# A long and a short product of each weight block, side by side instead of in two runs

## What is computed

```python
def _swiglu(x, w_gate, w_up, w_down):
    g = jnp.einsum('bsd,df->bsf', x, w_gate)
    u = jnp.einsum('bsd,df->bsf', x, w_up)
    return jnp.einsum('bsf,fd->bsd', jax.nn.silu(g) * u, w_down)

def first_block(x, ...):
    for layer in range(DEPTH):                 # DEPTH = 2
        ...
        x = _layer_norm(DEEPNORM_ALPHA * x + mix, ln1_g[layer], ln1_b[layer])
        ffn = _swiglu(x, ffn_w_gate[layer], ffn_w_up[layer], ffn_w_down[layer])
        x = _layer_norm(DEEPNORM_ALPHA * x + ffn, ln2_g[layer], ln2_b[layer])
    return x

def second_block(x, mem, ...):
    h = rms_norm(x, norm_g[layer])
    (qa, ka, va, ga, ub, vb, gb, qc, gc, ma, mb, mc) = split_cols(h @ w_in[layer], IN_SPLITS)
    ...
```

## Time and profile before

| | us |
|---|---|
| median of 3 runs | 916.92 |
| lowest and highest run | 916.55, 918.35 |
| span of the profiled execution | 915.3 |

### The profile page before, as it was taken

One profiled execution on the slowest core, in us unless ns is written; L12 is line 12 of the kernel. 1 busy time (PEld: TensorE's weight loads), 2 busy tenths in 40 slices (PEclk: granted clock), 3 DMA queues, 4 the chain that ended last, 5 costly groups with the idle time before them and its releaser, 6 DMA issues.

```text
span 915.3 us, 12823 instructions
## 1 busy us (share of the span) xinstructions
PE 907.1 (99%) x4764; PEld 764.0 (83%) x4764; DVE 610.7 (67%) x1004; ACT 508.4 (56%) x819; POOL 38.2 (4%) x50
## 2 busy tenths in 40 slices
PE   8999999999999999999999999999999999999997
PEld 7888788888888898878888888887888888888886
DVE  4897697776663756769776666376656577574665
ACT  5786555555552456666555555255557564655444
POOL 0100000450000001000000000001000000000000
PEclk9999999999999999999999999999999999999999
DMA  8854436677573577453855557354664565545551
GB/s 297 291 191 129 166 121 230 211 226 251 187 244 117 120 219 235 138 172 128 285 177 187 194 189 248 119 183 145 188 204 137 161 197 163 171 155 186 197 171 72
DMA packets 73036, 169.39 MB, mean 185 GB/s; under 512 B 11336, under 2 KB 33504, under 8 KB 72336
## 3 DMA queue, kind: packets, MB, share of 16 engines
q1 hardware_dynamic: 70512, 157.73, 53.3%
q0 software_dynamic: 2320, 10.58, 3.4%
q10 hardware_dynamic: 144, 0.26, 0.1%
HBM read 167.49 MB, written 1.06 MB: 184 GB/s over the span
## 4 chain that ended last, share of the span: by engine, by line
PE 97%; DMA 2%; ACT 1%; DVE 0%; SPq 0%; issue 0%; DVEq 0%; ACTq 0%
PE psum L789 21%; PE psum L976 15%; PE psum L695 8%; PE psum L697 8%; PE psum L700 8%; PE psum L980 7%; PE psum L1009 7%; PE psum L1014 3%; PE psum L900 3%; PE psum L910 3%; PE psum L904 3%; PE psum L1111 2%; PE psum L672 1%; PE psum L1142 1%; PE psum L1125 1%; DMA arena<-in_mem 1%
## 5 line engine op out<-in xcount | busy, mean ns | idle before, releaser
L1700 DVE TENSOR_TENSOR base_lo<-stage,base_hi 128x1024 fp32r<-128x1024 f32 (+3 forms) x222 | 262.0, 1205 | 95.1 <-ACT base_hi L1299 94.1
L1299 ACT CAST base_hi<-stage 128x1024 fp32r<-128x1024 f32 (+3 forms) x222 | 223.9, 1035 | 52.4 <-PE psum L700 22.5
L1700 DVE TENSOR_TENSOR extra_lo<-stage,extra_hi 128x1024 fp32r<-128x1024 f32 (+1 forms) x68 | 81.1, 1217 | 46.8 <-ACT extra_hi L1299 46.7
L695 PE MATMUL psum<-base_hi,xt 128*128 128x512 f32 (+2 forms) x256 | 100.7, 393 | 0.0
L697 PE MATMUL psum<-base_lo,xt 128*128 128x512 f32 (+2 forms) x256 | 98.3, 384 | 0.4 <-DVE base_lo L1700 0.4
L700 PE MATMUL psum<-base_hi,xt 128*128 128x512 f32 (+2 forms) x256 | 98.4, 385 | 0.0
L1299 ACT CAST extra_hi<-stage 128x1024 fp32r<-128x1024 f32 (+1 forms) x68 | 68.3, 1030 | 49.2 <-PE psum L789 31.6
L789 PE MATMUL psum<-base_hi,ht 128*128 128x512 f32 x288 | 87.3, 393 | 0.0
L976 PE MATMUL psum<-xt,extra_hi 128*128 128x512 f32 x320 | 87.3, 394 | 0.0
L1009 PE MATMUL psum<-xt,base_hi 128*128 128x512 f32 x240 | 76.5, 403 | 0.0
L976 PE MATMUL psum<-xt,base_hi 128*128 128x512 f32 x256 | 69.7, 394 | 0.0
(11 more groups left out here) (244 smaller groups left out, 1572.4 us busy)
## 6 DMA issues: line engine op xcount, KB each, us to landing
stage<-in_w_up SPq DMA_DIRECT2D x80, 512.0 KB, 4.4
stage<-in_w_down SPq DMA_DIRECT2D x44, 512.0 KB, 4.5
stage<-in_w_in_a SPq DMA_DIRECT2D x22, 512.0 KB, 5.2
stage<-in_w_cd_in SPq DMA_DIRECT2D x16, 512.0 KB, 4.6
stage<-in_w_in_b SPq DMA_DIRECT2D x12, 512.0 KB, 3.7
stage<-in_w_ab_in SPq DMA_DIRECT2D x11, 480.0 KB, 6.5
ln_par<-in_ln POOLq DMA_DIRECT2D x4, 1024.0 KB, 7.7
stage<-in_w_ab_out SPq DMA_DIRECT2D x8, 512.0 KB, 3.6
```

The costliest lines, as they stand in the source:

```text
L695: pe.matmul(acc, ah, wh, start=(k == 0), stop=False)
L1299: act.copy(w_hi(c, 0, w), stage_of(c, w)).then_inc(hi_done, 1)
L1700: dve.tensor_tensor(w_lo(c, 0, w), stage_of(c, w), w_hi(c, 0, w).bitcast(F32), ALU.subtract).then_inc(lo_done, 1)
```

## The change

In both functions the two inner loops change places. The outer one now runs over the blocks, and for each block the two kinds follow each other: long, short in the slices 0 to 6, short, long in the last one. No operation is added or left out; every matmul keeps its operands, its bank and its waits.

```diff
@@ step_by_hidden @@
                         for kk in range(g.kp):
                             k = m * g.kp + kk
-                            for high in ((True, False) if k < g.kc - 1 else (False, True)):
-                                for b in range(4):
+                            for b in range(4):
+                                for high in ((True, False) if k < g.kc - 1 else (False, True)):
                                     acc = (gates if b < 2 else ups)[:, b % 2, :]
                                     at = kk * g.n + b * P
@@ blocks @@
                         for kk in range(g.kp):
                             k = m * g.kp + kk
-                            for high in ((True, False) if k < g.kc - 1 else (False, True)):
-                                for b in range(2):
+                            for b in range(2):
+                                for high in ((True, False) if k < g.kc - 1 else (False, True)):
                                     acc, at = psum[:, 2 * (u % 2) + b, :], kk * g.n + b * P
```

## The result

The changed kernel takes 918.66 us (median of 20 runs, 917.83 to 921.24) against 917.21 us for the kernel before (20 runs beside them, 916.26 to 918.76). The ratio is 1.0019, with a 95% interval of 1.0013 to 1.0025: slower by some 1.5 us, where 1.9 us less were forecast. The time lies outside the range of the prediction. The difference isn't one of the clock: the 13 of these 20 runs with a mean granted clock of 0.999 or more average 918.56 us, and 27 such runs of the kernel before, made beside the first experiments, average 917.18.

A forecast was written before the change was run, and what follows sets the result against it. TensorE's fixed matmul list was taken as the bound. Savings of 1.4 us in `step_by_hidden` and 0.5 us in `blocks`, together 1.9, took the span from 915.3 to 913.4; with the median 1.6 above, 915.0 us, range 913.6 to 917.3.

The forecast's parts named there:

- What bounds the kernel: Whole kernel: TensorE's fixed list of matmuls sets the end, busy in 907.1 of 915.3 us and 97% of the chain.
- The number of operations: 576 long-short pairs in `step_by_hidden` and 272 in `blocks`, with none added or removed.
- the price of a pair before: Start to start in the old order: 350.3 ns in `step_by_hidden`, 349.7 ns in `blocks`.
- the steady prices: In runs of one kind, 226.7 ns for 512 columns and 120.0 ns for 256 columns, together 346.7 ns.
- What a pair will cost: Both functions: 347.9 ns, between 346.7 and 349.0; saves 1.4 us in `step_by_hidden` and 0.5 us in `blocks`.
- each long product pays: Rival for both functions: long products behind short ones make a pair 352.5 to 355 ns; 919.8 us, chance 0.1.
- all of the excess goes: Rival for both functions: a pair costs 346.7 ns or less, gain 2.9 us or more, 914.0 or below; chance 0.15.
- The edits at nothing: Side effects costed at zero: same PSUM bank twice running, earlier low-part wait, releases, and the start of a stretch.
- The bank: Neighbouring matmuls on one PSUM bank cost nothing; if wrong, 2 ns on each of 848 pairs, 1.7 us.
- wait for the low part: Comes 0.7 us earlier in `step_by_hidden` chunks, 0.23 us in `blocks`; 1.0 us of slack found, so no wait.
- the releases: Chunk and step ends still signal as before; other engines have 0.06 us less of 11.2 us per step.
- The Trainium skill's rule: Counterargument: weights load during the present matmul, so it costs its columns, a pair 325 ns in any order, no gain.

The follow-up runs named there:

- e4_uniform: Changed kernel with long, short also in the last slice of `step_by_hidden`, so no doubles there; 915.73 us against 917.23, ratio 0.9985.
- e11_two_two: Kernel before, with `step_by_hidden` in groups of two and two in place of four and four; 915.89 us against 916.98, ratio 0.9992.
- e3_extra_wait: Changed kernel with the already met wait for `turn_lo` repeated in all later turned steps; 919.02 us against 917.23, ratio 1.0017.
- e8_short_run: As e4_uniform, but each layer's first turned slice has four long, then four short products; run once, 914.99 us against 916.90.
- e10_first_swap: Kernel before with pairs without doubles in `step_by_hidden` and `in_ga`, one swap in each one's first slice; 915.75 us against 916.98, ratio 0.9987.
- e12_uniform_all: Kernel before with pairs without doubles in `step_by_hidden` and all of `blocks`; 916.16 us against 916.98, ratio 0.9995.
- e7_one_swap: As e4_uniform, but one short and one long product change places in slice 3 of every `step_by_hidden` step; 917.04 us against 916.90, ratio 1.0003.

## Why the prediction was wrong, point by point

- **What bounds the kernel** was right. The chain is TensorE's, and the difference in the time (1.45 us) is nearly the difference in the sums over its matmuls (1.36 us).
- **The number of operations** and the price of a pair before were right, and so were the steady prices whose sum is 346.7 ns.
- **What a pair will cost** is the step that failed. I put 347.9 ns, by halving the excess from four to two to one, with 349.0 ns as the upper end. Measured are 353.3 ns in most of `step_by_hidden` and 346.7 ns in its cheap parts. So it is no single price, and not between the bounds: the lower end is a true price, the upper end was none, and the dear state lies 4.3 ns above it. The prediction named a pair outside 346.7 to 349.0 ns as the sign of being wrong, and it came. The trace of before had a warning in it (a long product behind a short one costs 232.5 to 235 ns, a short one 118 to 120), and I used it only for a rival. An extrapolation over two run lengths was taken as the likeliest, though it says nothing about a pattern that the trace has nowhere. The reading at two and two was also a little high: 349.0 comes from rounded starts, by the unrounded ones the same five groups cost 348.4 ns a pair. That alone would have made the forecast lower still.
- **The rival "each long product pays"** had the right sign and nearly the right price, 353.5 ns against 353.3, and in part by luck. I gave it 0.1. Its mechanism, that a long product pays because it stands behind a short one, isn't what the runs show: in e4_uniform each long product stands behind a short one too, at 346.7 ns a pair. Nor are its parts right: in the dear state the long product costs 236.7 ns on the mean, not 232.5 to 235, and the short one 116.7, not 120. It put the time at 919.8; it came to 918.66, since a part of the stream is cheap: the stretch behind the transposes and one whole step in each layer, and some of `blocks`. My argument against it, that the pair had become cheaper from four to two while alternations doubled, was true (e11_two_two) and proved nothing about one and one.
- **The rival "all of the excess goes"** described what e4_uniform does behind the transposes. Its premise, that neither kind is ever in a run, isn't so in the changed kernel: there are doubles at the turn of each step. The section on the change has them in plain sight, and the prediction has no term for them, nor a reason to leave them out. Without them the pairs ahead of the transposes are dear all the same.
- **The edits at nothing** held. The bank costs nothing (e4_uniform), no wait for the low part came (the waits of after), the releases are as they were. An added wait that is met costs nothing either (e3_extra_wait).
- **The Trainium skill's rule** that a matmul costs its columns ("TensorE: Matmul & The Clock Gate", "Step-by-step: what each phase is for") says nothing of the order. For a pair it fits the mean of the cheap state to 0.1 ns if its fixed part is taken from this trace, 13.3 ns for each matmul. It doesn't cover the dear state: same matmuls, same order, 6.6 ns more for each pair. The formula N / 2.4 + 2.5, which the prediction took from "Back-to-back issue gap" of the same page of the Trainium skill, is given there for the gap of an isolated matmul, so its 325 ns was no figure for a stream with a weight load for each matmul.

**What stays open.** Why there are two states isn't shown. The runs show that they hold as long as nothing but pairs comes, that a stream behind a steady run of straight products of 512 columns starts dear and one behind the transposes starts cheap, and that a swap in midstream turns the state over. A stream can also start cheap behind straight products, if these are narrower: `cd_qk` begins behind products of 344 columns, in the changed kernel and in every other that has pairs there. In the changed kernel:

```profile
338.28 0.32 PE L700 MATMUL psum<-base_hi,xt 128*128 128x344 f32 x1
338.44 0.40 PE L1009 MATMUL psum<-xt,base_hi 128*128 128x512 f32 x1
...
339.14 0.39 PE L1009 MATMUL psum<-xt,base_hi 128*128 128x512 f32 x1
...
342.61 0.39 PE L1009 MATMUL psum<-xt,base_hi 128*128 128x512 f32 x1
```

From 339.14 to 342.61 ten pairs take 3.47 us, 347 ns each. In the changed kernel the doubles let the cheap state through at the end of the first turned step, lose it at the end of the second and leave the dear one as it is from then on. In `in_ga` they turn it over both ways: its three steps of 16 pairs cost 352.6, 347.2 and 352.8 ns a pair. What in the pattern makes the difference I didn't find, and behind straight products of 512 columns I found no way to start cheap either (e8_short_run, e10_first_swap).

## What to carry to other kernels

Where TensorE is busy all the time, the order of matmuls of different lengths is worth some nanoseconds each, and this is read from the distance of starts in the timeline, not from busy time. Don't extrapolate to an alternation that the trace doesn't have: bound it by the dearest neighbour rows, long behind short plus short ahead of long (here 235 + 120 = 355 ns, above the mean of 353.3), and give that end its weight. Strictly regular pairs, with no doubles where loops join, paid where the stream started cheap and was long (`step_by_hidden`, 200.04 us against 201.98); in `blocks` they were the dearest order (99.04 us against 98.25), and groups of two and two the best there. So look at what stands ahead of a stream, and at several steps before trusting one of them.

## What the runs showed of the hardware that I had not expected

- Two mean prices for the same alternating stream of a 512-column and a 256-column matmul: 346.7 and 353.3 ns for a pair, at a granted clock of 1.0 in both. The dear one is a cycle of three pairs, 350, 361 and 349 ns. The stream stayed dear for 48 pairs in `in_ga` (e12_uniform_all), to the end of the product, and cheap for 272 in each layer of e4_uniform.
- One exchange of two neighbours in 32 pairs turns the state over (e7_one_swap) and costs 1.65 us on the sum (201.69 against 200.04).
- The state at the start goes with what stands ahead: behind straight products of 512 columns the pairs start dear (353 ns), behind those of 344 columns cheap (347 ns). The latter is a single place in the program, and no run varies the columns alone.
- Two matmuls of a pair on the same bank cost nothing here: 346.6 ns in e4_uniform, against 346.7 for the sum of the steady prices.
- The distances repeat from layer to layer to within 2 ns in 100 us, so a single profiled execution settles a question that the times of a dozen runs, with intervals of 0.1%, can barely settle.
